# Output weight rows staged in the low-part slots, and the samples as third tile of the token-wise output projection, in a hybrid decoder step

## The reference, cut to what matters

```python
xn = rms_norm(h, n_mix_pre)
q, k, v, g, a, b = split(xn @ w_in)
o = retention(rotary(q), rotary(k), v)             # prompt: chunks of 128 with a state R; samples: one step from state_ret
ret_out = rms(o) * silu(g)                         # 4 heads of 128
conv_out = silu(layer_norm(depthwise_conv31(a * sigmoid(b))))      # 512 channels
mix = concatenate([ret_out, conv_out]) @ w_out     # 1024 x 1024
h = h + rms_norm(mix, n_mix_post)
xf = rms_norm(h, n_ffn_pre)
gate, up = split(xf @ w_ffn_in)                    # 2 x 2816
h = h + rms_norm((silu(gate) * up) @ w_ffn_out, n_ffn_post)
```

## Time and profile before

| what | value |
|---|---|
| median of three runs | 1179.01 us (1177.52 to 1179.39) |
| profiled execution, first to last instruction | 1177.5 us |
| PE busy | 1147.6 us (97%) |
| DVE busy | 802.6 us (68%) |
| POOL busy | 610.4 us (52%) |
| ACT busy | 444.1 us (38%) |
| chain that ended last, PE's share | 86% |

### The profile page before, as it was taken

One profiled execution on the slowest core, in us unless ns is written; L12 is line 12 of the kernel. 1 busy time (PEld: TensorE's weight loads), 2 busy tenths in 40 slices (PEclk: granted clock), 3 DMA queues, 4 the chain that ended last, 5 costly groups with the idle time before them and its releaser, 6 DMA issues.

```text
span 1177.5 us, 22875 instructions
## 1 busy us (share of the span) xinstructions
PE 1147.6 (97%) x8645; PEld 1127.8 (96%) x8645; DVE 802.6 (68%) x1242; ACT 444.1 (38%) x797; POOL 610.4 (52%) x457
## 2 busy tenths in 40 slices
PE   8999999999998999699999999999999999999997
PEld 7999999999998987699999999999999999999997
DVE  6458999854555237988585858584849585867646
ACT  6444444332343335542423333333333333333313
POOL 2066788304122347566565647474747373737316
PEclk9999999999999999899999999999999999999999
DMA  8411111112154223212121111212121212121134
GB/s 281 128 36 55 36 55 54 37 42 60 38 151 110 97 90 127 72 37 73 37 70 37 48 59 36 71 36 71 36 71 36 71 36 71 36 71 36 55 143 164
DMA packets 102360, 84.53 MB, mean 72 GB/s; under 512 B 2722, under 2 KB 89378, under 8 KB 102298
## 3 DMA queue, kind: packets, MB, share of 16 engines
q1 hardware_dynamic: 102258, 83.68, 22.9%
q10 hardware_dynamic: 48, 0.10, 0.0%
HBM read 72.86 MB, written 11.38 MB: 72 GB/s over the span
## 4 chain that ended last, share of the span: by engine, by line
PE 86%; DVE 5%; POOL 4%; issue 3%; DMA 1%; ACT 1%; DVEq 0%; SPq 0%; POOLq 0%; ACTq 0%
PE ps L410 27%; PE ps L412 27%; PE ps L411 27%; DVE w_ring L1611 1%; POOL o_last L837 1%; POOL h_ring L795 1%; DMA f_raw<-in_w_ffn_in 1%; PE ps L1801 1%; PE ps L1905 1%; POOL st L617 1%; PE ps L1924 1%; DMA gain_pre<-in_norm_mix_pre 1%; PE ps L2031 1%; PE ps L2030 1%; DVE x_lo L1605 0%
## 5 line engine op out<-in xcount | busy, mean ns | idle before, releaser
L1747 DVE TENSOR_TENSOR ffn_acc<-ps,ffn_acc 128x516 f32<-128x516 f32 x264 | 183.7, 696 | 7.9 <-PE ps L412 2.6
L410 PE MATMUL ps<-xn_hi,w_hi 128*128 128x350 f32 (+2 forms) x576 | 187.2, 325 | 1.1 <-DVE xn_lo L1306 1.1
L412 PE MATMUL ps<-xn_lo,w_hi 128*128 128x350 f32 (+2 forms) x576 | 185.2, 322 | 0.0
L411 PE MATMUL ps<-xn_hi,w_lo 128*128 128x350 f32 (+2 forms) x576 | 185.0, 321 | 0.0
L410 PE MATMUL ps<-x_hi,w_ring 128*128 128x256 f32 x616 | 175.2, 284 | 5.9 <-DVE e_s L1625 3.8
L410 PE MATMUL ps<-x,w_ring 128*128 128x260 f32 x616 | 175.4, 285 | 1.6 <-issue 1.2
L411 PE MATMUL ps<-x,w_ring 128*128 128x260 f32 x616 | 175.3, 285 | 0.0
L412 PE MATMUL ps<-x,w_ring 128*128 128x260 f32 x616 | 174.9, 284 | 0.0
L411 PE MATMUL ps<-x_hi,w_ring 128*128 128x256 f32 x616 | 173.9, 282 | 0.0
L412 PE MATMUL ps<-x_lo,w_ring 128*128 128x256 f32 x616 | 173.9, 282 | 0.0
L410 PE MATMUL ps<-act_hi,w_ring 128*128 128x258 f32 x560 | 158.2, 283 | 0.1
(11 more groups left out here) (256 smaller groups left out, 2670.6 us busy)
## 6 DMA issues: line engine op xcount, KB each, us to landing
f_raw<-in_w_ffn_in SPq DMA_DIRECT2D x42, 512.0 KB, 3.9
raw<-in_w_in SPq DMA_DIRECT2D x24, 512.0 KB, 3.8
f_raw<-in_w_ffn_out SPq DMA_DIRECT2D x22, 512.0 KB, 4.1
x_st<-in_x_prompt SPq DMA_DIRECT2D x8, 512.0 KB, 8.2
raw<-in_w_out SPq DMA_DIRECT2D x8, 512.0 KB, 6.4
h_ring<-in_x_prompt SPq DMA_DIRECT2D x8, 512.0 KB, 4.1
h_scratch<-h_ring SPq DMA_DIRECT2D x8, 512.0 KB, 3.1
h_fin<-h_scratch SPq DMA_DIRECT2D x8, 512.0 KB
```

What stands on the lines that cost most here:

```text
L410: nc.tensor.matmul(out, hi, mhi, start=first, stop=False, skip_group_check=resumes)
L411: nc.tensor.matmul(out, lo, mhi, start=False, stop=False, skip_group_check=resumes)
L412: return nc.tensor.matmul(out, hi, mlo, start=False, stop=last, skip_group_check=resumes)
L1747: v.tensor_tensor(a, tile_banks(i), a, ALU.add).then_inc(s_acc, 1)
```

## The change

1. **Staging.** The first three output weight units (24, 25, 26) are no longer loaded into `raw` but into the memory of `w_lo`, slots 0 to 2 (`wo_raw`), which is free as soon as the last gate jobs are through. Their loads wait neither for the stores of the states nor for the samples' outputs; they stand in SP's list behind the four stores. The hi split of these units reads `wo_raw`; the lo split reads it and overwrites it in place. Unit 27 keeps its place in `raw`. Units 28 to 30 are loaded into `raw` as soon as the states are stored and the hi splits of 24 to 26 done, ahead of the store of R; unit 31 follows that.
2. **ACT's order.** In chunk 5, the hi split of unit 24 stands ahead of `conv_hi(0)` and `ret_hi(0)`, and those of 25 and 26 behind them. Chunk 6 has none. DVE's order is unchanged.
3. **Tile order.** The token-wise projection takes the tiles in the order 0, 1, 8, 2, 3, 4, 5, 6, 7. All the steps, buffers and semaphores of the loop go by place instead of tile number, so that the sums of tile 1 are made at POOL step 3 and DVE step 4 as before, those of the samples at 4 and 5, of tile 3 at 6 and 7 (before: 5 and 6), of tile 5 at 8 and 9 (before: 7 and 8), of tile 7 at 10 and 11 (before: 9 and 10).
4. **Blocks.** The samples move to block x0, which has 260 columns, and x1 has 256. The addresses of the x blocks and of the samples' columns in the accumulator follow.

```diff
-SUBW = (2 * P, HALF - 2 * P)
+SUBW = (HALF - 2 * P, 2 * P)
+TILE_ORDER = (0, 1, 8, 2, 3, 4, 5, 6, 7)
+X_LAST = (1, 8, 3, 5, 7)
...
+        wo_raw = at("wo_raw", [P, 3, D], C + SLOTS * 4096 + SLOTS * 4096)
...
-            for r in range(SLOTS):
+            for r in range(3):
+                sp.wait_ge(s_job, 3 * N_IN - SLOTS + r + 1)
+                sp.dma_start(wo_raw[:, r, :].rearrange("p (k n) -> p k n", k=KT),
+                             w_out_v[:, :, r * P:(r + 1) * P]).then_inc(raw_in[r], 16)
+            sp.wait_ge(s_state[3], 32)
+            sp.wait_ge(s_os, SLOTS)
+            load_unit(3, w_out_v[:, :, 3 * P:4 * P], N_IN + SLOTS)
+            for r in range(3):
                 sp.wait_ge(s_state[r], 32)
-                sp.wait_ge(s_os, r + 1)
-                load_unit(r, w_out_v[:, :, r * P:(r + 1) * P], N_IN + r + 1)
+                sp.wait_ge(s_whi, N_IN + r + 1)
+                load_unit(r, w_out_v[:, :, (SLOTS + r) * P:(SLOTS + r + 1) * P], N_IN)
             sp.wait_ge(s_R, TILES + 1)
             sp.dma_start(ret_prompt[0, 0].rearrange("h d e -> d h e"), R[:, TILES % 2]).then_inc(s_rp, 16)
-            for r in range(SLOTS):
-                load_unit(r, w_out_v[:, :, (SLOTS + r) * P:(SLOTS + r + 1) * P], N_IN + SLOTS + r + 1)
+            load_unit(3, w_out_v[:, :, 7 * P:8 * P], N_IN + 2 * SLOTS)
...
             def w_split_hi(n):
+                src = wo_raw if N_IN <= n < N_IN + 3 else raw
...
-                s.copy(w_hi[:, n % SLOTS, :], raw[:, n % SLOTS, :]).then_inc(s_whi, 1)
+                s.copy(w_hi[:, n % SLOTS, :], src[:, n % SLOTS, :]).then_inc(s_whi, 1)
...
-                if n == 6:
-                    w_split_hi(N_IN)
                 if n == 7:
                     w_split_hi(N_IN + 3)
                 if n >= 1:
                     y_silu(n - 1)
-                if n == 6:
-                    w_split_hi(N_IN + 1)
...
                 if n == 6:
                     wo_evac(0)
-                    w_split_hi(N_IN + 2)
...
                 if n == 5:
+                    w_split_hi(N_IN)
                     conv_hi(0)
                     ret_hi(0)
+                    w_split_hi(N_IN + 1)
+                    w_split_hi(N_IN + 2)
...
-                if t == 10:
-                    x_sums_lo(7)
                 if 2 <= t <= 10:
-                    x_own_lo(t - 2)
-                if t in (4, 6, 8, 11):
-                    x_sums_lo(t - 3)
+                    x_own_lo(TILE_ORDER[t - 2])
+                if t >= 3 and TILE_ORDER[t - 3] in X_LAST:
+                    x_sums_lo(TILE_ORDER[t - 3])
...
-            def out_tok(t):
-
+            def out_tok(step):
+
+                t = TILE_ORDER[step]
...
-                    h_back(t - 2)
+                    h_back(TILE_ORDER[t - 2])
```

More of the change, by code:

```diff
@@ L267, in half_of, with place, pairs_before @@
         def half_of(t):
-            return (t % 2) * HALF + t // 2 * P + (2 if t // 2 == 3 else 0)
+            return (t % 2) * HALF + t // 2 * P + (4 if t // 2 >= 2 else 0)
+        def place(t):
+            return TILE_ORDER.index(t)
+        def pairs_before(t):
+            return 0 if t < 2 else 1 if t == TILES else t // 2 + 1
         def mix_pair(t):
-            return (2, 0, 1)[t % 3]
+            return (2, 0, 1)[place(t) % 3]
         def mix_cols(i):
@@ L384, in x_rows @@
                 return src
[L385 to L386 removed]
+            return src[:, :, 0:4] if first else src[:, :, 4:8]
         def w_slot(k, part):
@@ L533, in load_down_half @@
                                  "(e p) n -> p e n", p=P)).then_inc(fraw_in[slot], 16)
-            for t in range(3):
-                load_h(t)
-            for t in range(9):
+            for o in range(3):
+                load_h(o)
+            for o, t in enumerate(TILE_ORDER):
                 c0, n = OUT_TILES[t]
-                sp.wait_ge(s_h, t + 1)
-                sp.dma_start(h_scr[c0:c0 + n, :], h[t % 3][0:n, :]).then_inc(s_spill[t % 3], 16)
-                if 1 <= t and t + 2 < 9:
-                    sp.wait_ge(s_hs, t)
-                    sp.wait_ge(s_spill[(t - 1) % 3], 16 * ((t - 1) // 3 + 1))
-                    load_h(t + 2)
-                if t == 7:
+                sp.wait_ge(s_h, o + 1)
+                sp.dma_start(h_scr[c0:c0 + n, :], h[o % 3][0:n, :]).then_inc(s_spill[o % 3], 16)
+                if 1 <= o and o + 2 < 9:
+                    sp.wait_ge(s_hs, o)
+                    sp.wait_ge(s_spill[(o - 1) % 3], 16 * ((o - 1) // 3 + 1))
+                    load_h(o + 2)
+                if o == 7:
                     sp.wait_ge(s_T, 4)
@@ L785, in _ @@
             w_sums(0, 0, first=True)
-            for t in range(11):
-                if t < 9:
-                    mix_power(t)
-                if 1 <= t <= 9:
-                    h_power(t - 1)
-                if t < 9:
-                    n = OUT_TILES[t][1]
-                    pool.wait_ge(s_mg, t + 1)
-                    pool.wait_ge(s_h_in[t % 3], 16 * (t // 3 + 1))
-                    g.tensor_tensor(h[t % 3][0:n, :], h[t % 3][0:n, :], m_sc[0:n, :], ALU.add).then_inc(s_h, 1)
-                if t >= 2 and (t % 2 or t == 10):
-                    x_sums_14(t - 2)
+            for step in range(11):
+                if step < 9:
+                    mix_power(step)
+                if 1 <= step <= 9:
+                    h_power(step - 1)
+                if step < 9:
+                    n = OUT_TILES[TILE_ORDER[step]][1]
+                    pool.wait_ge(s_mg, step + 1)
+                    pool.wait_ge(s_h_in[step % 3], 16 * (step // 3 + 1))
+                    g.tensor_tensor(h[step % 3][0:n, :], h[step % 3][0:n, :], m_sc[0:n, :], ALU.add).then_inc(s_h, 1)
+                if step >= 2 and TILE_ORDER[step - 2] in X_LAST:
+                    x_sums_14(TILE_ORDER[step - 2])
             def ffn_group(gg, first=False):
```

167 lines of the change are left out of this document (86 added, 81 removed).

## The result

| | before | changed |
|---|---|---|
| median of the runs | 1178.4 us (1177.0 to 1179.4, 8 runs) | 1182.5 us (1181.1 to 1185.7, 8 runs) |
| ratio | | **1.0039**, 95% interval 1.003 to 1.0047 |
| span of the profiled execution | 1177.5 us | 1181.5 us |

The account below looks back on a forecast made before the run. The prediction took PE, busy 1147.6 of 1177.5 us, as the bound, with only its gaps and slow clock to win. Part A +2.0 and part B +2.1 gave +4.1 on 1179.0, so 1183.1 us, range 1177.1 to 1186.4.

Parts of the forecast that it names:

- part A: Staging and ACT's order, up to TensorE's job 0: job 0 starts late, +2.0 us, between +0.3 and +3.6.
- part B: Tile order in the token-wise loop: +2.1 us on VectorE's line, bounds -2.15 and +3.8.
- the wait for the load: ACT's hi split of unit 24 waits for its weights ahead of `ret_hi(0)`: 1.0 us, bounds 0 and 1.7.
- The clock term: Slow clock at job 0, losing 1.7 us before: change taken as 0, between -0.7 and +0.9.
- the prediction's dearer case: Behind job 0's longer gap, the slow clock goes on about twice as long: +0.9 us.
- the shift of the loop up to m_sc at place 8: Token-wise loop: m_sc(8) comes at 477.7 instead of 478.60, a gain of 0.9 us.
- content and blocking behind it: VectorE from m_sc(8) on: +0.95 us of changed work, +2.05 of standing still beside POOL and idling.
- what TensorE feels: Product 1 of x1 waits for tile 7's first lo, 500.8 against 499.65; product 3 for a `u2` 2.1 us late.
- Rival 1: End of the loop: PE, not DVE, sets it; part B -5.8, part A +2.0, so 1175.2 us; chance 0.13.
- Rival 2: Both parts near nothing: part A +0.3 to +1, part B +0.5 to +1, about 1180.5 us; chance 0.27.
- Rival 3: Slow clock twice, behind the gaps ahead of job 0 and product 1: +3.6 and +3.8, 1186.4 us; chance 0.12.
- Rival 4: The staging does nothing, since DVE's order and not the load held job 0; no chance of its own.

Follow-up runs that it names:

- b_small: `b_only` with POOL's two sums for tiles 5 and 7 cut to 4 of 128 columns, part of the computation left out; 0.9978 to the kernel before.
- u2_fill: The kernel before with 32 transposes of the identity ahead of TensorE's product k = -4, in its longest pause (3.8 us for `u2`); 1.0002.
- before_small: The kernel before with POOL's two sums for tiles 5 and 7 cut to 4 of 128 columns, part of the computation left out; 1.0000.
- a_behind: The kernel before with the staging's early loads, but ACT makes `conv_hi(0)` and `ret_hi(0)` ahead of all three weight splits; 1.0002.
- b_only: The kernel before with the new tile order and blocks alone (points 3 and 4 of the change); 1.001.
- ret_first: The kernel before with `ret_hi(0)` ahead of `conv_hi(0)` on ACT and `w_lo(24)` ahead of mask and k on VectorE; 0.9987.
- lo_first: The kernel before with one edit on VectorE: the lo split of unit 24 ahead of mask and k of chunk 7; 0.9975.
- a_only: The kernel before with the staging and ACT's new order alone (points 1 and 2 of the change); 1.0037.

## Why the prediction was right, and where its steps were off

Forecast 1183.1 us and slower by over 0.2%; measured 1182.5. The sum was 4.1, measured 4.6 (3.5 to 5.5). The mechanisms are those that the prediction names, but that the sum came so near is partly luck: part A was put 1.0 us too low and part B 0.6 too high, and TensorE got its share of part B in another way than forecast.

**Part A, forecast +2.0, traced +3.0, alone 4.4 (2.7 to 6.0).** The chain from `ret_hi(0)` over `ret_lo(0)`, mask, k and `w_lo` to job 0 is right link by link, and the split cost its 1.0. The term that was mis-sized is the wait for the load: 1.0 was taken, 1.74 measured. The upper bound was 347.7 for the landing; the changed kernel has 346.8, or 347.8 with the 1.0 of its early start. Counted from `y_norm(5)`, the load was issued 1.0 us earlier than the first one before and landed at the same time. The argument for a value inside the bounds was weak: if the stores and the load ahead of it are the same in both kernels, that argues for the bound itself. The ring order that the Trainium skill describes in "DMA: Bandwidth & Descriptors", "Queues, rings and completion order" gave this end, and this trace agrees with it, though it doesn't show single rings. The clock term was taken as 0 and came out as (3.7 - 3.4) / 2 = 0.15. The slow stretch did last twice as long, the prediction's dearer case, but it began in the pause, which the prediction hadn't thought of.

**Part B, forecast +2.1, traced +1.5, alone 1.2 (0 to 2.4).** Three terms, one by one:

- the shift of the loop up to m_sc at place 8: -0.9 forecast, -1.4 measured. The step from place 5 was put at 6.2 us (460.9 after 454.69) and took 5.99; the one from 7 to 8 was put at 9.0 and took 8.80; place 6 to 7 at 7.8, took 7.75. This is the term that was mis-sized;
- content and blocking behind it: +0.95 and +2.05 forecast. From the m_sc at place 8 to the end of the last lo of sums it is 24.0 us now (479.19 to 503.19) and was 21.1: +2.9, where +3.0 was forecast. Splits of k = -4, -3 and -2 were put at 0.35, 1.2 and 0.85 over the free 0.68 and took 0.26, 1.07 and 0.73; the pair of k = 1 and 2 was put at 1.85 and took 1.8 more than in `b_small`. The 0.26 of k = -4 is there in `b_small` too, so it isn't these sums';
- what TensorE feels: the forecast put product 1 1.15 us late (500.8 against 499.65) and the `u2` behind it 2.1 late, for which product 3 would wait. It was 0.65 and 1.55, both 0.5 less for the shift. But TensorE never waited for that `u2`: product 3 starts at 506.45, 0.8 behind its end, since the clock was low from 503.6 on. The forecast put this slow stretch at 0. The 0.85 us behind product 1 were lost in it; without it TensorE would probably have waited for VectorE, as it does in `b_small`, and how much less would then have been lost isn't shown.

The exclusive lock that the Trainium skill describes in "SBUF — State Buffer", "Who interferes with whom" holds in each of these rows: 1.75 instead of 0.70 beside POOL, not a third more.

**The rivals.** Rival 1 (TensorE the bound) is refuted by `u2_fill` and by `b_small`; its condition, that POOL leave the splits alone, was right as a statement: with it the tile order is 2.6 us faster (0.9978, where `before_small` has 1.0000). Rival 2 didn't come: neither term of part A was small. Rival 3, the slow clock twice, came as a mechanism and not at its price. Behind job 0 the stretch was twice as long, but cost 0.15 more. Behind product 1 it came as rival 3 says (0.50 from 503.6 to 507.0), but what was lost there against the kernel before is the 0.85 named above, not 1.7. There is one more, from 497 to 500, behind the 2.2 us wait for `act2`; the 2.0 us wait ahead of product 1 comes after it, so a faster TensorE would only have waited longer there. Rival 4 is true of the early loads, as `a_behind` shows.

**What stays open.** Part A's time alone is 4.4 us with 2.7 as its lower end; its traces show 3.0 and 3.1. The difference isn't outside the interval. One source of it can be named but not weighed: the trace of the kernel before has the slow stretch behind job 0, those of `before_small` and `u2_fill` have not, and against them the m_sc at place 3 is 4.6 to 4.7 us later with the staging instead of 3.0 to 3.1. In how many executions the stretch comes isn't known. No run takes the slow stretch behind product 1 by itself. And `before_small` leaves open why the old order gains nothing at all.

## What to carry to other kernels

Before a step is moved ahead on an engine, look at what stands right behind it there and who waits for that: here one cast of 1.0 us and its wait for a load went ahead of two casts that GpSimd, VectorE and, behind them, TensorE were waiting for. When two engines exclude each other, an instruction has to be placed by what the other engine does at that moment; the same split cost 1.2 or 3.7 us by where it stood, and a tile order that is 2.6 us faster when POOL's sums are cut short is 1.2 slower with them whole. And a term that depends on the clock can be there in one execution and not in the next, so one trace doesn't price it. The best edit was the smallest: two casts moved into idle time of ACT, without any new load, gave 3.7 us.

## What the runs showed of the hardware

- **A small POOL instruction isn't cheap beside a busy VectorE.** In the changed kernel the samples' two sums, 16 elements wide, took 1.20 and 1.19 us; in `before_small`, where nothing was in their way, instructions of the same size took 0.22:

```profile
453.64 1.20 POOL L722 TENSOR_TENSOR x_sum<-x_sum,x_a 128x16 f32<-128x16 f32 x1
```
```profile
487.96 0.22 POOL L706 TENSOR_TENSOR x_f<-x_a,x_f 128x16 f32<-128x16 f32 x1
```

- **The length of one pause doesn't tell whether the clock falls.** Ahead of job 0 the kernel before, `b_only`, `a_behind`, `b_small`, `before_small` and `u2_fill` pause for 2.37 to 2.40 us, and all but `a_behind` run the same instructions up to there. In one profiled execution of each, the granted clock behind it was 0.50 for about 3.4 us in the first four and stayed at 1.00 in the last two. Behind 2.15 us in `b_only` it was 0.65 from 492 to 496, and behind 2.16 us in `b_small`, at the same place of the list, it stayed at 1.00 throughout. Behind a pause of 1.69 and of 1.21 us (`ret_first`, `lo_first`) it stayed at 1.00, in one execution each. Behind 5.2 us it fell in both traces that have that pause (`a_only` and the changed kernel).
